# A Trainium2 block kernel: the first norm's weight row turned by itself, x and the weights first in the DMA queues, the small loads behind them, the identity turned meanwhile

## What is computed

```python
h = rmsnorm(x, norm_mix_pre[l])
proj = h @ w_in[l]
xr, yr, q, k, v, g_rnn, g_attn = jnp.split(proj, IN_OFFSETS, axis=-1)
...
q = rope(q.reshape(B, S, N_Q_HEADS, HEAD_DIM), positions)
k = rope(k.reshape(B, S, N_KV_HEADS, HEAD_DIM), positions)
```

## Time and profile before

| | |
|---|---|
| median of 3 runs | 2317.41 us (2316.6 to 2319.15) |
| the profiled execution | 2315.3 us, its span 2313.6 us |
| PE busy | 2252.5 us, 97% |
| DVE, ACT, POOL busy | 62%, 52%, 17% |
| mean granted TensorE clock | 0.996 |
| DMA | 427.01 MB, mean 185 GB/s |
| the chain that ended last | PE 82%, DVE 9%, ACT 3%, issue 3%, DMA 2%, POOL 1% |

### The profile page before, as it was taken

The page is one execution under the profiler, slowest core; times in us unless marked ns, Lnnn a source line. Parts: engine busy times, 40 slices in busy tenths (PEclk is TensorE's granted clock), DMA queues, the critical chain, the costliest instruction groups (busy, mean ns, idle before and its releaser), DMA issues.

```text
span 2313.6 us, 32956 instructions
## 1 busy us (share of the span) xinstructions
PE 2252.5 (97%) x11754; PEld 1893.6 (82%) x11754; DVE 1429.7 (62%) x1625; ACT 1197.5 (52%) x1851; POOL 383.3 (17%) x408
## 2 busy tenths in 40 slices
PE   7999999999999999999999999998999999999999
PEld 6888899788888778888888888888977778888887
DVE  6666657644554575555555555566799977675554
ACT  5555557544444446555555555555444445554442
POOL 2133440000000102212122121211243311110000
PEclk9999999999999999999999999999999999999999
DMA  8544454566666846666666666665566655556655
GB/s 246 166 140 138 140 151 149 174 190 192 190 190 193 262 157 199 201 204 205 196 204 201 194 208 201 197 206 171 178 177 182 186 172 170 164 164 188 187 189 163
DMA packets 215027, 427.01 MB, mean 185 GB/s; under 512 B 14032, under 2 KB 14320, under 8 KB 214384
## 3 DMA queue, kind: packets, MB, share of 16 engines
q1 hardware_dynamic: 206720, 398.51, 56.3%
q0 software_dynamic: 7744, 26.62, 3.6%
q10 hardware_dynamic: 432, 0.13, 0.0%
HBM read 414.71 MB, written 10.49 MB: 184 GB/s over the span
## 4 chain that ended last, share of the span: by engine, by line
PE 82%; DVE 9%; ACT 3%; issue 3%; DMA 2%; POOL 1%; SPq 0%; ACTq 0%; DVEq 0%
PE acc L1855 23%; PE acc L1857 23%; PE acc L1856 22%; PE acc L1847 3%; PE acc L1849 3%; PE acc L1850 3%; DVE w_lo L1149 3%; PE tps L1870 1%; DMA raw<-in_w_out_dram 1%; ACT w_hi L660 1%; DMA raw<-in_w_in_dram 1%; PE tps L1976 1%; PE sides L1976 1%; PE sides L1926 1%; POOL tmp L577 1%
## 5 line engine op out<-in xcount | busy, mean ns | idle before, releaser
L1149 DVE TENSOR_TENSOR w_lo<-raw,w_hi 128x1024 fp32r<-128x1024 f32 x752 | 938.7, 1252 | 769.1 <-ACT w_hi L660 764.4
L660 ACT ACTIVATE w_hi<-raw 128x1024 fp32r<-128x1024 f32 x752 | 794.4, 1059 | 905.6 <-PE acc L1857 746.1
L1855 PE MATMUL acc<-w_hi,h_hi 128*128 128x512 f32 x1440 | 572.8, 398 | 6.9 <-DVE w_lo L1149 5.8
L1857 PE MATMUL acc<-w_hi,h_lo 128*128 128x512 f32 x1440 | 562.8, 391 | 0.0
L1856 PE MATMUL acc<-w_lo,h_hi 128*128 128x512 f32 x1440 | 561.9, 390 | 0.0
L1855 PEld LDWEIGHTS acc<-w_hi,h_hi 128*128 128x128 f32 x1440 | 271.2, 188 | 75.0 <-issue 15.8
L1857 PEld LDWEIGHTS acc<-w_hi,h_lo 128*128 128x128 f32 x1440 | 271.0, 188 | 57.8
L1856 PEld LDWEIGHTS acc<-w_lo,h_hi 128*128 128x128 f32 x1440 | 271.4, 188 | 53.2
L1855 PE MATMUL acc<-w_hi,slab_dg_r 128*128 128x512 f32 x768 | 300.1, 391 | 3.9 <-DVE w_lo L1149 3.9
L1857 PE MATMUL acc<-w_hi,slab_dg_r 128*128 128x512 f32 x768 | 299.3, 390 | 0.0
L1856 PE MATMUL acc<-w_lo,slab_dg_r 128*128 128x512 f32 x768 | 299.3, 390 | 0.0
(11 more groups left out here) (371 smaller groups left out, 2315.1 us busy)
## 6 DMA issues: line engine op xcount, KB each, us to landing
raw<-in_w_in_dram SPq DMA_DIRECT2D x328, 512.0 KB, 3.8
raw<-in_w_mlp_up_dram SPq DMA_DIRECT2D x128, 512.0 KB, 3.8
raw<-in_w_mlp_down_dram SPq DMA_DIRECT2D x128, 512.0 KB, 4.7
raw<-in_w_out_dram SPq DMA_DIRECT2D x64, 512.0 KB, 4.6
raw<-in_w_rnn_proj_dram SPq DMA_DIRECT2D x32, 512.0 KB, 4.4
raw<-in_w_attn_proj_dram SPq DMA_DIRECT2D x32, 512.0 KB, 3.9
trig_scratch<-tmp POOLq DMA_DIRECT2D x32, 256.0 KB, 4.3
raw<-in_w_proj_ssm_dram SPq DMA_DIRECT2D x16, 512.0 KB, 3.8
```

Source lines behind the costliest of these rows:

```text
L660: nc.scalar.activation(w_hi[:, j % RING], raw[:, j % RING], ACT.Copy).then_inc(hi_ready, 1)
L1149: V.tensor_tensor(w_lo[:, j % RING], raw[:, j % RING], w_hi[:, j % RING].bitcast(F32), ALU.subtract)\
L1855: T.matmul(o, hi[:, k, c], wh, start=first, stop=False)
L1857: ins = T.matmul(o, lo[:, k, c], wh, start=False, stop=last)
```

## The change

- ACT issues the norm's weight row first, with a semaphore of its own (`gain_landed`); PE turns it alone (16 columns), and ACT copies only that before the first `x_high`. The four other rows of the first tile stay behind it on ACT's queue and are turned in step 2. The seven rows of the second tile go to SP's queue behind the fourth weight piece and are turned in step 3.
- POOL builds its masks and constants first, then waits until the last chunk of x has landed, then issues the four rotary loads. The ten lambda loads come behind the rstd, ahead of the loads of the recurrence's gate weights.
- The first x chunk is scaled and split in halves, with a weight split behind each half. `x_low` tells PE of its first half (`x_half_lo`), so an even step starts on half a chunk; this holds at all three norms.
- PE turns the identity 10, 8 and 6 times (`keep_turning`) ahead of and between the first turns.
- Hooks: DVE's angles from place 3 to 4, cosines from 6 to 7; the lambda sums, a hook of their own now, to place 3 of the q unit; `softplus` from place 2 to 5 there. ACT: sines from 5 to 6, exponentials from place 1 to 4 of the q unit.

```diff
+        def load_rows(eng, rows, tile, landed):
...
             for s in range(LEAD, S):
                 load(w_in, slice(o_k, o_k + NC), 2 * s, U_KV * S + s, s)
+                if s == LEAD:
+                    load_rows(sp, SECOND_ROWS, 1, rows_landed[1])
...
+            pool.wait_ge(x_landed[NH - 1], 16)
             pool.dma_start(freq[:], inv_freq.rearrange("(o f) -> o f", o=1).broadcast_to([P, 32])).then_inc(side_landed, 16)
...
                 pool.tensor_tensor(small[:, 6:8], small[:, 4:6], neg_half[:, 0:2], ALU.pow).then_inc(rstd_ready, 1)
                 if n == 0:
+                    load_lambda()
...
+            load_rows(act, FIRST_ROWS[:1], 0, gain_landed)
+            load_rows(act, OTHER_ROWS, 0, rows_landed[0])
...
-            x_high(0, 0, mix_gain)
-            split_hi(None, 0, 0, 0)
-            split_hi(None, 0, 0, 1)
+            for half in range(2):
+                x_high(0, 0, mix_gain, (half,))
+                split_hi(None, 0, 0, half)
...
-            hooks[2].append(lambda: pt_copy_(1))
-            hooks[5] = [rotary_sines]
+            hooks[2].append(lambda: pt_copy_(0))
+            hooks[3].append(lambda: pt_copy_(1))
+            hooks[6] = [rotary_sines]
...
-            steps(None, 0, U_QX * S, {1: [exponentials], 3: [lambda: row_copy(1)], 5: [k_copy]})
+            steps(None, 0, U_QX * S, {3: [lambda: row_copy(1)], 4: [exponentials], 5: [k_copy]})
...
-                ins.then_inc(tps_free, 1)
+                    ins.then_inc((x_half_lo, tps_free)[half], 1)
...
-            hooks = {3: [rotary_angles], 5: [lambda: mean_square(NH, 1)], 6: [cosines_and_lambda]}
+            hooks = {4: [rotary_angles], 5: [lambda: mean_square(NH, 1)], 7: [cosines]}
...
-            steps(None, 0, U_QX * S, {2: [softplus]})
+            steps(None, 0, U_QX * S, {3: [lambdas], 5: [softplus]})
...
+            def keep_turning(times):
+                for n in range(times):
+                    T.transpose(side[1][:, n % 4 * P:(n % 4 + 1) * P], ident[:, :], ident[:, :])
...
+                half0 = {0: 0, T_MLP_IN: NH, T_N2: 2 * NH}[t0]
+                at = {2 * c: [lambda c=c: pe.wait_ge(x_half_lo, half0 + c + 1)] for c in range(NH)}
+                for c in range(NH):
+                    at[2 * c + 1] = [lambda c=c: pe.wait_ge(tps_free, t0 + c + 1)]
...
-            turn_rows(0)
-            for c in range(2):
-                turn_x(c, 0, None)
+            keep_turning(10)
+            turn_gain()
+            keep_turning(8)
+            turn_x(0, 0, None)
+            keep_turning(6)
+            turn_x(1, 0, None)
```

More of the change, by code:

```diff
@@ L358, in griffin_block_then_ssm_block @@
         block = ctx.enter_context(nc.Block())
+        def load_rows(eng, rows, tile, landed):
+            at = sum(n for _, n in FIRST_ROWS[:1]) if rows is OTHER_ROWS else 0
+            for name, n in rows:
+                src = a[name]
+                if name == "conv_w":
+                    src = src[0].rearrange("w (r c) -> (w r) c", c=P)
+                elif len(src.shape) == 3:
+                    src = src[0].rearrange("(r g) s -> r (g s)", g=2)
+                else:
+                    src = src[0].rearrange("(r c) -> r c", c=P)
+                eng.dma_start(stg[at:at + n, tile, 0:P], src).then_inc(landed, 16)
+                at += n
         @block.sync
@@ L680, in evac_hi, with x_high @@
                 ins.then_inc(tps_hi, 1)
[L683 to L694, removed]
-            def pt_copy_(n):
[L697 to L701, removed]
+            load_rows(act, FIRST_ROWS[:1], 0, gain_landed)
+            load_rows(act, OTHER_ROWS, 0, rows_landed[0])
+            def pt_copy_(n):
+                act.wait_ge(pt_ready, n + 2)
+                at = ((KT, P), (0, P))[n]
+                nc.scalar.activation((pt1, pt2)[n][:, at[0]:at[1]], acc[1][:, (1 - n) * NC + at[0]:(1 - n) * NC + at[1]],
+                                     ACT.Copy).then_inc(cols_ready, 1)
+            def x_high(c, t0, col, halves=(0, 1)):
+                for half in halves:
                     if half:
@@ L1188, in reduce_angle, with x_low @@
                 return V.tensor_scalar(r, r, SAFE_PI, -SAFE_PI, ALU.min, ALU.max)
-            def x_low(c, hi_index, col):
-                for half in range(2):
+            def x_low(c, hi_index, col, halves=(0, 1)):
+                for half in halves:
                     if half:
@@ L1290, in _ @@
             dve.wait_ge(cols_ready, 1)
-            x_low(0, H_X, mix_gain)
-            split_lo(None, 0, 0, 0)
-            split_lo(None, 0, 0, 1)
+            for half in range(2):
+                x_low(0, H_X, mix_gain, (half,))
+                split_lo(None, 0, 0, half)
             x_low(1, H_X, mix_gain)
             split_lo(None, 0, 0, 2)
-            hooks = {3: [rotary_angles], 5: [lambda: mean_square(NH, 1)], 6: [cosines_and_lambda]}
+            hooks = {4: [rotary_angles], 5: [lambda: mean_square(NH, 1)], 7: [cosines]}
             for c in range(2, NH):
@@ L1302, in _ @@
             dve.wait_ge(v_ready, 1)
+            chain.wait()
             for t in range(TT):
@@ L1891, in turn_rows @@
             def turn_rows(n):
[L1892 to L1893 removed]
+                pe.wait_ge(rows_landed[n], 16 * len((OTHER_ROWS, SECOND_ROWS)[n]))
+                T.transpose(acc[1][:, (1 - n) * NC:(1 - n) * NC + P], stg[:, n, 0:P], ident[:, :]).then_inc(pt_ready, 1)
             def x_as_it_comes(t0, first_x):
[L1897 to L1899 removed]
+                half0 = {0: 0, T_MLP_IN: NH, T_N2: 2 * NH}[t0]
+                at = {2 * c: [lambda c=c: pe.wait_ge(x_half_lo, half0 + c + 1)] for c in range(NH)}
+                for c in range(NH):
+                    at[2 * c + 1] = [lambda c=c: pe.wait_ge(tps_free, t0 + c + 1)]
+                    if c < NH - 2:
+                        at[2 * c + 1].append(lambda c=c: turn_x(c + 2, t0, first_x))
                 return at
@@ L1908, in rstd_row, with turn_gain @@
                 ins.then_inc(row_ready, 1)
-            turn_rows(0)
-            for c in range(2):
-                turn_x(c, 0, None)
-            unit(None, 0, U_KV * S, 0, U_KV, h_hi, h_lo, hooks={4: [lambda: turn_rows(1)]},
+            def turn_gain():
+                pe.wait_ge(gain_landed, 16)
+                T.transpose(acc[1][:, 0:KT], stg[0:KT, 0, 0:P], ident[0:KT, 0:KT]).then_inc(pt_ready, 1)
+            keep_turning(10)
[4 more added lines that the diff above has]
+            turn_x(1, 0, None)
+            unit(None, 0, U_KV * S, 0, U_KV, h_hi, h_lo, hooks={4: [lambda: turn_rows(0)], 6: [lambda: turn_rows(1)]},
                  before=x_as_it_comes(0, None))
-            pe.wait_ge(cols_ready, 2)
+            pe.wait_ge(cols_ready, 3)
             def attention(i, c):
```

40 lines of the change are left out of this document (23 added, 17 removed).

## The result

The changed kernel takes 2321.97 us (median of 19 runs, 2318.72 to 2329.59); the kernel before took 2317.22 beside it (19 runs, 2315.08 to 2319.27). The ratio is 1.0023, 95% interval 1.0016 to 1.0031: slower by some 5 us. The forecast was 2312.4, range 2309.6 to 2316.4. The sign is wrong.

What follows compares the result with a forecast made beforehand. PE, busy in 97% of a 2313.6 us span, was taken to bound the kernel. Terms -4.6, -1.6, -0.3, -0.1, -0.4, +2.0 sum to -5.0: 2315.3 us profiled becomes 2310.3, plus 2.1 for the median is 2312.4, range 2309.6 to 2316.4.

Steps and rivals of the forecast that it cites:

- Start, -4.6: Start of the kernel: step 0's first product begins at 10.4 instead of 14.97, gaining 4.6 us.
- step 2, -1.6: Early steps: step 2's weight piece is split in time, so PE doesn't wait ahead of step 2, gaining 1.6 us more.
- The wait of 0.77 ahead of step 4 stays: Ahead of step 4: PE's 0.77 us wait remains, as turning x3, scaling and splitting keep their order.
- The turn of q, +2.0, bounds 0.6 to 3.5: End of the q unit: PE newly waits for the rotation of q, costing 2.0 us, bounds 0.6 to 3.5.
- I take 6.2: q unit: step 15's weight piece takes 6.2 us to load, between 4.7 freely and 7.6 beside the gate weights, landing at 50.1.
- the gate weights starve steps 14 to 17: Late steps: sign of being wrong, the gate weights, now later, starve these steps; no size given.
- The lambda loads, 6.5 us, landed 47.5: q unit: ten issues end at 41.5 and a load takes 6.5 us, landing at 47.5, so the sums run to 49.3.
- rival 5: q unit: the last lambda load lands 9.2 us after issue or later; 2314.4 at 9.2 us; chance 0.14.
- The clock: Near 65 us: sign of being wrong, a PE wait brings the granted clock under 1.00; no term in the sum.
- Later norms, -0.4: Two later norms: steps starting on half a chunk gain 0.4 us of PE's waits of 0.23 and 0.33.
- step 7, -0.3: Ahead of step 7: DVE's angles move behind lo 7, so PE's wait of 0.17 goes, gaining 0.3 us start to start.

Runs made afterwards that it cites:

- both: Changed kernel with the lambda loads directly behind the rotary loads and the gate weights held until PE is through the first q unit; ratio to before 0.9975.
- gatelate: Changed kernel with only the gate weights held until PE is through the first q unit, lambda loads left behind the rstd; 2319.17 us.
- lam17: Changed kernel with the ten lambda loads issued directly behind the four rotary loads, gate weights not held; 2315.79 us.
- lamearly: Changed kernel with the ten lambda loads issued near 4 us, ahead of the wait for x, gate weights not held; 2319.29 us.
- hooksonly: Kernel before with only the change's new hook places, all loads where they were; ratio to before 1.0004 to 1.0021.

## Why the prediction was wrong

*Start, -4.6, and step 2, -1.6.* Right: 5.0, and no wait ahead of step 2. Landings, bandwidth and the early clock came as worked out. From both one sees that these terms reach the end: without the wait at the turn of q the sum is -7.0, and the kernel both measured -6.3.

*The wait of 0.77 ahead of step 4 stays.* It was 0.64.

*The turn of q, +2.0, bounds 0.6 to 3.5.* This is the step that failed. The chain was the right one, and its length too: from lo 16 at 53.9 I had 12.7 us to the turn of q at 66.6 (its terms, 1.2, 4.9, 2.3 and 4.1, add up to 12.5); the trace shows 12.54. But lo 16 began at 60.35, 6.4 us later. The error is in "I take 6.2" for the piece of step 15, with 7.6 as the upper bound, and in a quick piece of step 16 behind it. Measured: 12.1 and 14.7. Step 15's piece landed at 55.6 instead of 50.1, and ACT waited 0.85 more for step 16's. The bound was taken from the earlier trace rows, a piece beside the gate weights alone. Here the lambda loads stand directly ahead of the gate weights in POOL's queue, and SP's pieces meet both. gatelate and lam17 show that it took both: 8.4 us for step 15's piece beside the lambda loads alone, 8.0 beside the gate weights alone. The prediction did name it as a sign of being wrong that the gate weights starve steps 14 to 17, but with no time in the sum. The lambda loads' price had been seen in the earlier trace rows, share 1.06 at 103 GB/s; it was credited where the loads left and not debited where they went. PE's waits came to 6.5 us, not 2, the first of them (2.41) for lo 15, where the forecast had none.

*The lambda loads, 6.5 us, landed 47.5.* The last took 9.6 and landed at 51.05. That was rival 5, priced at 2314.4 through the chain of the sums alone. But what decided lay in SP's queue: even with the sums waiting until 51.1, lo 16 could have started at about 55.5 (sums 1.6, exponentials 1.6, hi 16 1.1, by the lengths of the forecast), had its piece been there. gatelate comes near that case: its last lambda load lands at 50.07, and lo 16 starts at 55.21.

*The clock.* It was named as what would make the forecast wrong, and was no term of the sum. In each of the seven kernels in which PE waited over 2 us between 60 and 76 us, the trace has a half-clock stretch of 3.4 us or more in that part (0.91 or less from 62 to 80); in each of the seven without such a wait it has none from 62 to 120. A stretch costs 3.4 x 0.5 = 1.7 us. So of the 8.7 us, 6.5 are waits and 1.7 the clock; the half us left is not accounted for. After the turn of q another 2.8 us are lost to the end of the span (4.6 - 1.8). Counted in both traces from 76 us on, the stretches at half clock add up to 27.4 us with the change, one at 132.5 among them, and 20.6 before. By the same sum that costs 3.4 us more, while the later norms give 1.1 back (next paragraph): the sizes fit to about half a us. But where such later stretches fall differs between all the kernels, and no run sets them apart, so this cause is not shown.

*Later norms, -0.4, and step 7, -0.3.* The medians can't tell these, but the traces show them. From the first turn of x to the first product the two later norms took 3.86 us each before and 3.31 and 3.33 with the change: 1.1 us gained in all, not 0.4. The wait of 0.17 ahead of step 7 is gone.

What the runs show of the whole: the change as made +4.8; lambda loads early -6.5; gate weights held as well a further -4.6; that is both, at -6.3. These two collisions are the bill, and neither touches the start.

## What to carry to other kernels

A small load that is moved doesn't lose its price (the packets of the five dear loads took 0.66 us each where they stood before, from 11 to 20 us, and 0.96 where they went): work out how much of the DMA engines' *time* it takes where it stands now, and look at which transfer's landing falls there. For a loop that loads each piece only when a buffer comes free, a piece that is 5 us late is passed on through every engine. And do not join two chains that both have slack: softplus behind lo 16 cost nothing until lo 16 was late. Where a gain at the start doesn't arrive at the end, look for the first wait behind it, not for an error in the start.

## What the hardware showed

- Copying one 256-byte row to 128 partitions can take the DMA engines ten times as long as the same bytes from 128 different rows: 0.96 us of an engine for a packet of 2048 bytes against 0.095, which is also what a packet of that size takes for the weights (0.098). The Trainium skill, "DMA: Bandwidth & Descriptors", Why small descriptors are slow (HBM only), gives descriptors of 256 bytes an overhead of 27%; here 256-byte pieces were no burden with different sources, so size isn't what costs. That a row is repeated is not enough either. In gatelate `sub_gain`'s load copies one row of 512 bytes to 128 partitions, and its 16 packets of 4096 bytes took 0.17 us each; of the 80 dear packets there the first 16 took 0.11 us on average and the last 16 took 1.41. Whether it is the row's length, its place in memory or several such loads at once, no run sets apart.
- Two queues with work do not always share the engines evenly: 98.3% against 1.6% of the time in the changed kernel from 43 to 47 us. It doesn't take the dear packets. In lam17 the lambda loads had landed by 30 us; with gate weights alone in POOL's queue, and the pieces of steps 14 and 15 waiting in SP's, the queues from 44.5 to 45.5 us were:

```profile
q0 software_dynamic: 99, 0.33, 99.6%
q1 hardware_dynamic: 9, 0.02, 5.1%
```

The same page of the Trainium skill, Queues, rings and completion order, says that an engine goes round-robin between its queues by packets. From 51 to 54 us the changed kernel's trace agrees, with 208 packets of POOL's queue and 216 of SP's; in the two stretches above it doesn't, and no run here explains that.
- The granted clock fell to half behind a wait of 2.06 us in lam17, lamearly and hooksonly, in hooksonly on a PE that had not waited since 30.8 us. It did not behind the wait of 2.41 ahead of 57.97 in the changed kernel, nor behind one of 2.59 ahead of 24.57 in lamearly. So the length of a wait alone doesn't decide, and a wait of this size carries a risk of 1.7 us more.
